# A macaron encoder layer on one core: softmax maxima and sums in one tile, new transpose banks, all attention scaling on VectorE

## The chip, the cores and the metric

The kernel is one launch on one core of a Trainium2 chip. The metric is device time in microseconds, the median of several runs. Engines are named PE (TensorE), DVE (VectorE), ACT (ScalarE), POOL (GpSimd) and SP (SyncE, which only starts transfers); PEld is the weight load of PE. Each has its own instruction queue and they meet by semaphores. All arithmetic is float32: a product of two float32 matrices is made as three passes over parts rounded to fp32r, high by high, high by low and low by high. So every operand of a product is first copied by ACT to its high part ("hi") and then subtracted by DVE to give its low part ("lo").

## The reference

```
x = x + 0.5 * post1(SwiGLU_1(pre1(x)))
h = pre_mix(x); z = h @ w_in            # pool channels | q | k | v
mixer A: centred pooling, windows 2, 4, 8, 16, minus the token, small matrix per group, scale
mixer B: dilated sliding-window attention, 3 groups of 4 heads,
         (window, dilation) = (128,1), (512,4), (2048,16), ALiBi bias
x = x + post_mix(concat(A, B) @ w_out)
x = x + 0.5 * post2(SwiGLU_2(pre2(x)))

# of one group g:
m = max(s); p = exp(s - m); den = sum(p); o = (p @ v) / den; lse = m + log(den)
# over the groups:
alpha = softmax(lse over the 3 groups); output of g = o_g * alpha_g
```

Sequence 1024, width 1024, 12 heads of 64, FFN width 2752; `post` and `pre` are RMS norms with a gain.

## The kernel before, in words

The stages follow one another: the first FFN (`gate_up(0)`, `down(0)`, up to about 625 us), the input projection in two halves of the sequence (`project_in(0)`, `project_in(1)`), the attention, the output projection, and the second FFN (`gate_up(1)`, `down(1)`). PE never waits for a stage as a whole; every engine has its list of work written out by hand, and the same lists are walked on PE, DVE and ACT.

**Attention.** There are 24 tiles n of 128 queries, 8 for each group. Tile n goes through: scores on PE (L2228), bias and maxima on DVE (`maxima`, L1500 and L1506), exponentials and their sums on ACT (`exps`, L1022), transpose on PE (`turn`, L2243), copy out of PSUM by DVE or ACT (L1519, L1032), values on PE (`values`, L2260), copy out by DVE (L1511). The maxima stand in `m_neg`, the sums in `den`, one column for a tile and head. ("step", n) in a list means: transpose tile n-2, scores of tile n, values of tile n-3. `SCHEDULE` puts steps 0 to 18 inside and behind the units of the second half of the input projection; `AFTER_IN` holds what comes behind it, steps 19 to 26 among it.

**The joint softmax.** Groups 1 and 2 have their tokens in another order, so their maxima and sums are transposed to rows, put back in natural order by the copy (`rows_`), and transposed back ("stat", b on PE L2270, its copy at L1016 or L1492, then "nat", k on PE L2312, copies at L1559 and L1560). From `nat` the coefficients follow (L1569 to L1592), those of groups 1 and 2 are transposed forth and back again (L2325, L2335), and `scale_out` (L529) multiplies the values `o_all` (a part of `vT`), once for each pair of heads and group: two by DVE, four by POOL. `turn_outputs` (L2345) transposes the scaled values; ACT and DVE copy them to `mixT`.

**Banks.** Every transpose, pool product and turned output b has a number, a PSUM bank (`TR_BANK`) and a copying engine (`TR_ON_DVE`, the others are ACT's). `tr_bank(b)` on PE waits until the last earlier b of the same bank has been copied.

**Output projection.** 24 units n, 8 slices of `w_out` for 2, then 3, then 3 tiles of tokens. For each: `hi_proj` on ACT (L720), `out_x_hi` on ACT (L1076, `mhi`), `out_w_lo` (L1193) and `out_x_lo` (L1620, `mlo`) on DVE, then 12 or 18 matmuls (L2362 to L2364) on PE. Inside these units ACT, DVE and POOL norm the finished tiles 0 to 4; `OUT_SQ1`, `OUT_NEW`, `OUT_SQ2`, `OUT_NORM` and `OUT_TURN` say behind which unit. `OUT_TURN` places the transposes `turn_x` of tiles 0 to 3 on PE (L1942), all into banks 6 and 7; ACT copies them (L784, L791) and DVE subtracts (`x_lo`, L1231) before the next may use the banks.

**Start of an FFN.** `first_steps` on DVE: weights (`lo_g`, L1175) and the four instructions of `split` for a tile (L1241 twice, L1244, L1246).

Of the kernel before, what the change touches and what calls it, by code (L numbers as in the profile page):

```python
# [6 lines left out]
F32 = mybir.dt.float32  # L7
F32R = mybir.dt.float32r
ALU = mybir.AluOpType
# [3 lines left out]
P = 128  # L13
# [121 lines left out]
OUT_SQ1, OUT_NEW, OUT_SQ2 = (7, 9, 16, 17, 19), (8, 10, 17, 18, 20), (9, 11, 18, 19, 21)  # L135
OUT_NORM, OUT_TURN = (10, 12, 19, 20, 22), (12, 15, 21, 22)
# [19 lines left out]
    (18, "mid"): [("step", 15)], (18, "end"): [("stat", 12), ("step", 16)],  # L156
    (19, "mid"): [("outw", 0), ("stat", 13), ("step", 17)], (19, "end"): [("stat", 14), ("step", 18)],
}
AFTER_IN = [("stat", 15), ("v", 12), ("step", 19), ("v", 13), ("pool", 0), ("step", 20), ("v", 14), ("pool", 1),
            ("step", 21), ("v", 15), ("pool", 2), ("pool", 3), ("step", 22), ("stat", 24), ("stat", 25), ("step", 23),  # L160
            ("nat", 0), ("step", 24), ("stat", 27), ("stat", 28), ("step", 25), ("outx", 0), ("nat", 1), ("step", 26),
            ("unit", 0)]

SCORES_FIRST = 19

# [5 lines left out]
V_NO, POOL_NO = (*range(12), 16, 17, 19, 21), (18, 20, 22, 23)  # L171
STAT_NO = {12: (1, 0, 0), 13: (1, 0, 1), 14: (1, 1, 0), 15: (1, 1, 1), 24: (2, 0, 0), 25: (2, 1, 0), 27: (2, 0, 1), 28: (2, 1, 1)}
TR_NAT, TR_ROWS, TR_COEF, TR_END = (26, 29), 30, 36, 47
TURNED_IN = {2: (34, 35), 3: (37, 38), 4: (39, 40), 5: (41, 42), 6: (43, 44), 7: (45, 46)}
TR_BANK = [4 + b % 4 for b in range(8)] + [7] * 9 + [5, 7, 5, 7, 5, 7, 5, 7, 5, 7, 5, 7, 5] + [6, 7, 4, 5] + [6, 7, 4]\
    + [5, 6, 7, 4, 5, 6, 7, 4, 5, 6]
TR_ON_DVE = (1, 3, 5, 7, 9, 11, 16, 21, 26, 28, 29, 35, 36, 38, 42, 46)
# [33 lines left out]
def layer_program(nc, io, out, xs1, xs2):  # L211
    hd = nc.dram_tensor("hd_dram", (PROD, PAIRS, P, HALF), F32).ap()
    ctx = ExitStack()
    with ctx:
# [20 lines left out]
        m_neg = sb("m_neg", [P, NTILES * HPG])  # L235
        den = sb("den", [P, NTILES * HPG])
# [61 lines left out]
        rows_ = [over(96, "rows1", [HPG, 2, SEQ]), over(0, "rows2", [HPG, 2, SEQ])]  # L298
# [213 lines left out]
        def copy_stat(copy, b):  # L512
            g, s, c = STAT_NO[b]
            copy(b, natural(rows_[g - 1][:, s, :], g, c), as_permuted(ps[0:HPG, TR_BANK[b], :], g))

        def copy_coef_rows(copy, b):
            g, c = 1 + (b - TR_ROWS) // 2, (b - TR_ROWS) % 2
            copy(b, *own_half(rows_[g - 1][:, 0, :], ps[0:HPG, TR_BANK[b], :], g, c))
# [149 lines left out]
        def _(act):  # L668
# [349 lines left out]
            def exps(n):  # L1018
                act.wait_ge(smax_done, n + 1)
                nk = P if n >= 2 * NT else 2 * P  # L1020
                for h in range(HPG):
                    a = act.activation(probs[:, n % 2, h, 0:nk], probs[:, n % 2, h, 0:nk], ACT.Exp,  # L1022
                                       bias=m_neg[:, n * HPG + h:n * HPG + h + 1],
                                       accum_out=den[:, n * HPG + h:n * HPG + h + 1])
                a.then_inc(exp_done, 1)

            def items(todo):
                for what, n in todo:
# [8 lines left out]
                    elif what == "outx":  # L1037
# [16 lines left out]
            def joint_softmax():  # L1054
                out_hi(1)
                act.wait_ge(stat_step, STAT_EXP)
                e = nat[:, 0, :, :].rearrange("p g n -> p (g n)")
                act.activation(e, e, ACT.Exp).then_inc(stat_exp, 1)
                hi_proj(OUT_U0 + 2)
# [4 lines left out]
                copy_turned(3)  # L1064
                for l in range(4, OUT_UNITS):
                    out_hi(l - 1)
                    copy_turned(l)

# [21 lines left out]
            def project_out():  # L1090
                x_load(R_MIX)
                x_load(R_MIX + 1)
                for n in range(3 * OUT_UNITS - 1):
                    if n % OUT_UNITS == OUT_UNITS - 1:
                        evac_mix(n // OUT_UNITS)
                    for i in range(HT):
# [3 lines left out]
                    if OUT_EARLY <= n + 2 < 3 * OUT_UNITS:  # L1100
                        out_hi(n + 2)
# [61 lines left out]
        def _(dve):  # L1163
# [70 lines left out]
            def split(p, i):  # L1234
# [4 lines left out]
                hi = x_split(q, 0)  # L1239
                for b, dst in enumerate(x_split(q, 1)):  # L1240
# [1202 lines left out]
```

## Time and profile before

| | |
|---|---|
| runs | 1730.39, 1730.68, 1732.2 us; median 1730.68 |
| profiled execution, its own time | 1730.15 us |
| its span | 1728.3 us, mean granted clock 0.995 |
| PE busy | 1692.5 us, 98% |
| DVE, ACT, POOL busy | 65%, 42%, 36% |

PE is busy nearly everywhere, so only three things can move the time: matmuls left out, places where PE stands still, and stretches in which its clock is halved. A busy time of the page counts an instruction's tail, which overlaps the next one: two matmuls of 512 columns start 0.227 us apart though one is given 0.39 us, and two 128-column transposes start 0.109 us apart though one is given 0.27 us. In a timeline row the number before the engine is the length of the row and the bracket gives the idle time before it and what ended it.

### The profile page before, as it was taken

How to read it: one execution, taken by the hardware profiler on the slowest of the kernel's cores; microseconds unless marked ns; L12 is line 12 of the kernel's file. 1: busy time of each engine (PE TensorE's matmuls, PEld its weight loads, DVE VectorE, ACT ScalarE, POOL GpSimd, SP SyncE). 2: the span in 40 equal slices, each digit the busy share in tenths (PEclk: the TensorE clock that was granted, in tenths of full speed). 3: DMA queues.
4: the chain of work that ended last, by engine and by line, in shares of the span. 5: the costliest groups of instructions: out<-in, count | busy, mean ns of one | idle time of the engine just before them, and what ended most of it. 6: DMA issues, size and time to landing. Idle time of an engine off the chain costs nothing. (4 is left out here: it accounts for less than half of the span.)

```text
span 1728.3 us, 21686 instructions
## 1 busy us (share of the span) xinstructions
PE 1692.5 (98%) x7949; PEld 1402.2 (81%) x7949; DVE 1116.0 (65%) x1405; ACT 717.4 (42%) x1264; POOL 621.4 (36%) x489
## 2 busy tenths in 40 slices
PE   7999999999999999999999998999999999999997
PEld 6888888888888888887887887788888888888886
DVE  7866665665668784424555767877656556647877
ACT  7432333332444553334445566533333323344453
POOL 3465554543352111118010111446545445345111
PEclk9999999999999999999999999999999999999999
DMA  6132233233853455332110256322342233484362
GB/s 216 64 116 92 92 118 132 92 100 115 316 180 101 140 152 170 119 92 84 50 50 25 67 202 183 107 88 92 111 138 93 94 114 110 152 289 144 98 232 92
DMA packets 160985, 216.98 MB, mean 126 GB/s; under 512 B 12848, under 2 KB 99056, under 8 KB 160880
## 3 DMA queue, kind: packets, MB, share of 16 engines
q1 hardware_dynamic: 153136, 188.73, 34.2%
q10 hardware_dynamic: 6896, 24.19, 4.0%
q0 software_dynamic: 848, 2.69, 0.5%
q8 instruction: 64, 1.05, 0.3%
q14 instruction: 41, 0.34, 0.1%
HBM read 162.09 MB, written 52.95 MB: 124 GB/s over the span
## 5 line engine op out<-in xcount | busy, mean ns | idle before, releaser
L2057 PE MATMUL ps<-xg,ring 128*128 128x512 f32 x1120 | 436.4, 390 | 2.3 <-DVE ring L1175 1.7
L2059 PE MATMUL ps<-xg,ring 128*128 128x512 f32 x1120 | 435.8, 389 | 0.0
L2058 PE MATMUL ps<-xg,ring 128*128 128x512 f32 x1120 | 435.7, 389 | 0.0
L2057 PEld LDWEIGHTS ps<-xg,ring 128*128 128x128 f32 x1120 | 210.2, 188 | 47.5 <-DVE ring L1175 2.5
L2059 PEld LDWEIGHTS ps<-xg,ring 128*128 128x128 f32 x1120 | 210.2, 188 | 44.0
L2058 PEld LDWEIGHTS ps<-xg,ring 128*128 128x128 f32 x1120 | 210.2, 188 | 43.1
L2120 PE MATMUL ps<-ring 128*128 128x512 f32 x616 | 240.3, 390 | 0.8 <-DVE ring L1187 0.8
L2122 PE MATMUL ps<-ring 128*128 128x512 f32 x616 | 239.7, 389 | 0.0
L2121 PE MATMUL ps<-ring 128*128 128x512 f32 x616 | 239.7, 389 | 0.0
L691 ACT ACTIVATE ring<-t_sum 128x512 fp32r<-128x512 f32 x160 | 100.3, 630 | 278.6 <-PE ps L2059 168.5
L1193 DVE TENSOR_TENSOR ring<-raw,ring 128x1024 fp32r<-128x1024 f32 x64 | 82.2, 1284 | 152.4 <-ACT ring L720 152.3
L1175 DVE TENSOR_TENSOR ring<-t_sum,ring 128x512 fp32r<-128x512 f32 x160 | 151.6, 957 | 17.9 <-ACT ring L691 17.8
L1756 POOL TENSOR_TENSOR t_sum<-raw 128x512 f32<-128x512 f32 x80 | 112.8, 1429 | 131.0 <-DVE ring L1175 114.9
L1723 POOL TENSOR_SCALAR ms<-ss 128x1 f32<-128x1 f32 x44 | 23.0, 523 | 328.7 <-ACT junk_d L755 113.1
L1778 POOL TENSOR_TENSOR u_a<-hst 128x512 f32<-128x512 f32 x40 | 66.1, 1653 | 204.5 <-DVE hst L1302 204.5
L1184 DVE TENSOR_TENSOR ring<-st_op,ring 128x1024 fp32r<-128x1024 f32 x66 | 103.9, 1574 | 51.4 <-ACT ring L702 51.2
L2120 PEld LDWEIGHTS ps<-ring 128*128 128x128 f32 x616 | 115.6, 188 | 26.0 <-DVE ring L1187 1.9
L2122 PEld LDWEIGHTS ps<-ring 128*128 128x128 f32 x616 | 115.6, 188 | 24.0
L2121 PEld LDWEIGHTS ps<-ring 128*128 128x128 f32 x616 | 115.6, 188 | 23.6
L1175 DVE TENSOR_TENSOR ring<-raw,ring 128x512 fp32r<-128x512 f32 x120 | 128.7, 1073 | 3.1 <-ACT ring L691 3.1
L2150 PE MATMUL ps<-xe,ring 128*128 128x512 f32 x320 | 127.5, 399 | 0.0
L2152 PE MATMUL ps<-xe,ring 128*128 128x512 f32 x320 | 124.9, 390 | 0.0
(220 smaller groups left out, 2781.1 us busy)
## 6 DMA issues: line engine op xcount, KB each, us to landing
st_op<-hd_dram SPq DMA_DIRECT2D x154, 256.0 KB, 2.7
raw<-in_w_gate_dram SPq DMA_DIRECT2D x20, 1024.0 KB, 6.3
raw<-in_w_up_dram SPq DMA_DIRECT2D x20, 1024.0 KB, 5.4
raw<-in_w_in_dram SPq DMA_DIRECT2D x40, 512.0 KB, 3.8
hd_dram<-u_b SPq DMA_DIRECT2D x64, 256.0 KB, 6.3
wd<-in_w_down_dram SPq DMA_DIRECT2D x18, 768.0 KB, 7.0
hd_dram<-hst SPq DMA_DIRECT2D x48, 256.0 KB, 6.3
raw<-in_w_out_dram SPq DMA_DIRECT2D x24, 512.0 KB, 3.6
```

The source lines that it names most:

```text
L691: act.activation(small(m % RING, 0), src, ACT.Copy).then_inc(hi_done, 4 if m == M_FRONT - 1 else 1)
L1175: dve.tensor_tensor(small(m % RING, 1), src, small(m % RING, 0).bitcast(F32), ALU.subtract)\
L1184: a = dve.tensor_tensor(lo, src, hi.bitcast(F32), ALU.subtract)
L1756: pool.tensor_tensor(t_tile(n, t), x, y, ALU.subtract).then_inc(t_done, 1)
L2057: pe.matmul(acc, hi[:, a, :], x_hi, start=(a == 0 and not more), stop=False, skip_group_check=more)
L2058: pe.matmul(acc, hi[:, a, :], x_lo, start=False, stop=False, skip_group_check=more)
L2059: mm = pe.matmul(acc, lo[:, a, :], x_hi, start=False, stop=(a == HALF_D - 1), skip_group_check=more)
L2120: pe.matmul(acc, s_hi, w_hi, start=(j == 0 and not top), stop=False, skip_group_check=top)
L2121: pe.matmul(acc, s_hi, w_lo, start=False, stop=False, skip_group_check=top)
L2122: return pe.matmul(acc, s_lo, w_hi, start=False, stop=(j == PAIRS - 1), skip_group_check=top)
L2150: pe.matmul(ps[:, bank, :], hi[:, a, :], x_hi, start=(a == 0), stop=False)
L2152: mm = pe.matmul(ps[:, bank, :], lo[:, a, :], x_hi, start=False, stop=(a == DT - 1))
```

## The change

1. `m_neg` and `den` become one tile `stats[P, tile, 2, head]`. One transpose carries the maxima and the sums of a tile, so that 8 "stat" entries with 4 transposes each become 4, and each "nat" has 8 transposes of 8 rows where it had 16 of 4 rows.
2. All numbers b, the banks and the copying engines are laid out anew, and `AFTER_IN` is in another order. ("stat", 15) in front of ("v", 12) is gone; there now stand ("outw", 1), DVE's and ACT's share of the weights of output unit 1, and ("nat", 0). The three parts of ("outx", 0) become ("xh", 0) on ACT and ("xl", 0) on DVE, ("unit", 0) moves ahead of step 24, and unit 1 runs between `turn_outputs(2)` and `turn_coefficients_back`.
3. The values of the last two tiles are copied by ACT (`LAST_VALUES`).
4. All six `scale_out` are on DVE, one behind each of the output units' work.
5. `OUT_*` move: tile 1 one unit earlier, the transposes of tiles 1 and 2 one unit earlier, tile 4 later; POOL works out its factors in the order 0, 1 then 2, 3 then 4.
6. At the start of an FFN `split` of the second tile is cut in two with `lo_g(p, 1)` between, and PE's unit (1, 0) waits only for the first half of it.

```diff
-OUT_SQ1, OUT_NEW, OUT_SQ2 = (7, 9, 16, 17, 19), (8, 10, 17, 18, 20), (9, 11, 18, 19, 21)
-OUT_NORM, OUT_TURN = (10, 12, 19, 20, 22), (12, 15, 21, 22)
+OUT_SQ1, OUT_NEW, OUT_SQ2 = (7, 8, 16, 17, 19), (8, 9, 17, 18, 21), (9, 10, 18, 19, 22)
+OUT_NORM, OUT_TURN = (10, 11, 19, 20), (12, 14, 20, 22)
...
-AFTER_IN = [("stat", 15), ("v", 12), ("step", 19), ("v", 13), ("pool", 0), ("step", 20), ("v", 14), ("pool", 1),
...
+AFTER_IN = [("outw", 1), ("nat", 0), ("v", 12), ("step", 19), ("v", 13), ("pool", 0), ("step", 20), ("v", 14), ("pool", 1),
+            ("step", 21), ("xh", 0), ("v", 15), ("pool", 2), ("step", 22), ("xl", 0), ("pool", 3), ("stat", 23),
+            ("step", 23), ("unit", 0), ("stat", 24), ("xh", 1), ("step", 24), ("nat", 1), ("step", 25), ("step", 26)]
...
-        m_neg = sb("m_neg", [P, NTILES * HPG])
-        den = sb("den", [P, NTILES * HPG])
+        stats = sb("stats", [P, NTILES, 2, HPG])
...
             def joint_softmax():          # ACT
-                out_hi(1)
                 act.wait_ge(stat_step, STAT_EXP)
...
+                for n in range(NTILES - LAST_VALUES, NTILES):
+                    act.wait_ge(pv_done, n + 1)
+                    act.activation(o_all[:, n, :], ps[:, 6, 0:HPG * HEAD], ACT.Copy).then_inc(o_done, 1)
...
                 scale_out(dve, 0, 0).then_inc(scaled, 1)      # DVE
+                out_x_lo(1)
                 scale_out(dve, 0, 1).then_inc(scaled, 1)
...
+                tr_copied(dve, TR_COEF)
+                scale_out(dve, 1, 0).then_inc(scaled, 1)
+                for l in range(3, OUT_UNITS):
+                    out_w_lo(l)
+                    copy_turned(l)
+                    if l < OUT_UNITS - 1:
+                        out_x_lo(l)
+                    if l < OUT_UNITS - 2:
+                        scale_out(dve, *divmod(l, 2)).then_inc(scaled, 1)
...
-            for g in (1, 2):              # POOL
-                for w in (0, 1):
-                    scale_out(pool, g, w).then_inc(scaled, 1)
...
                 split(p, 0)
-                split(p, 1)
+                split_first(p, 1)
                 lo_g(p, 1)
+                split_rest(p, 1)
...
                     if (n, k) == (1, 0):
-                        pe.wait_ge(xlo_done, Q_FFN[p] + HT + 2)
+                        pe.wait_ge(s3_done, HT * p + 2)
...
             def turn_stat(b):
...
-                    mm = pe.transpose(ps[0:HPG, bank, T * P:(T + 1) * P], (m_neg, den)[s][:, n:n + HPG], ident[:, :])
+                    mm = pe.transpose(ps[0:2 * HPG, bank, T * P:(T + 1) * P],
+                                      stats[:, n, :, :].rearrange("p s h -> p (s h)"), ident[:, :])
```

What this does to the queues, at two places. On PE, behind the second half of the input projection, the rows before are (v is `vT`, one row for four transposes; the first row is ("stat", 15)):

```order
L2270 MATMUL ps<-ident,den 4x128 x4
L2195 MATMUL ps<-ident,vT 128x128 x4
L2243 MATMUL ps<-ident,probs 128x128 x4
```

At the same place and at the end of `AFTER_IN` after the change the last statistics and the joint softmax stand like this, with unit 0 (12 rows of L2379 to L2381) just ahead of the first row:

```order
L2284 MATMUL ps<-ident,stats 8x128 x4
L2257 MATMUL ps<-ident,probs 128x128 x4
L2274 MATMUL ps<-v_nat,probsT 128x64 x4
L2326 MATMUL ps<-ident,rows 128x8 x8
L2257 MATMUL ps<-ident,probs 128x128 x4
L2274 MATMUL ps<-v_nat,probsT 128x64 x8
L2339 MATMUL ps<-ident,nat 4x128 x16
L2359 MATMUL ps<-ident,vT 128x128 x8
```

The transpose of sums that stood in front of the value transposes is gone, the transposes back are 8 and not 16, and an output unit stands among the statistics.

On DVE, from the first scaling on, before:

```order
L529 TENSOR_TENSOR vT<-vT,coef 128x8x128 x2
L1193 TENSOR_TENSOR ring<-raw,ring 128x1024
L1620 TENSOR_TENSOR mlo<-mixT,mhi 128x256
L1193 TENSOR_TENSOR ring<-raw,ring 128x1024
L1492 COPY mixT<-ps 128x512
L1492 COPY coef<-ps 128x64
L1620 TENSOR_TENSOR mlo<-mixT,mhi 128x256
L1492 COPY mixT<-ps 128x512
```

and after the change, from the copy of the coefficients (`coef`) on, two output units' worth:

```order
L1505 COPY coef<-ps 128x64
L528 TENSOR_TENSOR vT<-vT,coef 128x8x128
L1196 TENSOR_TENSOR ring<-raw,ring 128x1024
L1505 COPY mixT<-ps 128x512
L1634 TENSOR_TENSOR mlo<-mixT,mhi 128x256
L528 TENSOR_TENSOR vT<-vT,coef 128x8x128
L1196 TENSOR_TENSOR ring<-raw,ring 128x1024
L1505 COPY mixT<-ps 128x2x256
L1634 TENSOR_TENSOR mlo<-mixT,mhi 128x256
L528 TENSOR_TENSOR vT<-vT,coef 128x8x128
```

Each output unit now has four instructions in DVE's queue, weights, copy of a turned output, low part, and a scaling, where it had three at most.

## Rows read from the trace of the kernel before

**Rows 1.** The profile's page: busy time, share of the span, instructions.

```profile
PE 1692.5 (98%) x7949; PEld 1402.2 (81%) x7949; DVE 1116.0 (65%) x1405; ACT 717.4 (42%) x1264; POOL 621.4 (36%) x489
```

**Rows 2.** Waits of PE: in total, times, longest (us).

```profile
PE ps L2195 <- ACT rows L1016: 4.0, 1, 4.0
PE ps L1942 <- DVE xg L1231: 3.6, 1, 3.6
PE ps L2362 <- DVE mlo L1620: 2.1, 3, 1.2
PE ps L2057 <- DVE ring L1175: 1.7, 1, 1.7
```

**Rows 3.** Stretches of the span: length, busy time by engine, granted clock (PEclk), DMA.

```profile
943.00:990.00 47.00, 41.80 (x315) 36.21 (x314) 31.85 (x77) 26.41 (x78) 4.63 (x4) 0.93 0.19 57
...
950.60:954.02 3.42, 2.87 (x14) 2.90 (x15) 1.38 (x2) 0.41 (x1) 0.00 (x0) 0.50 0.00 0
954.02:977.92 23.90, 22.80 (x193) 19.83 (x193) 17.47 (x51) 15.96 (x54) 0.00 (x0) 1.00 0.02 3
977.92:981.33 3.41, 3.41 (x9) 2.65 (x9) 3.20 (x9) 0.90 (x1) 1.16 (x2) 0.50 0.82 222
1076.90:1080.32 3.42, 3.42 (x12) 2.83 (x11) 0.42 (x1) 2.53 (x4) 0.00 (x0) 0.50 0.07 26
```

**Rows 4.** A group of PE instructions between 943 and 990 us.

```profile
L2312 PE MATMUL ps<-ident,rows 4*128 4x4 f32 x32 | 2.2, 197 | 0.5 <-ACT rows L1016 0.5
```

**Rows 5.** Timeline behind the input projection: start, length, engine, instruction, idle before.

```profile
943.02 0.60 PE L2270 MATMUL ps<-ident,den 128*4 128x128 f32 x4
943.46 0.60 PE L2243 MATMUL ps<-ident,probs 128*128 128x128 f32 x4
...
948.41 0.40 ACT L1022 ACTIVATE probs<-probs,m_neg 128x128 f32<-128x128 f32 x1 [3.21 <-DVE m_neg L1506]
949.97 1.04 ACT L1016 ACTIVATE rows<-ps 4x512 f32<-4x512 f32 x1
951.15 1.09 PE L2195 MATMUL ps<-ident,vT 128*128 128x128 f32 x4 [3.98 <-ACT rows L1016]
952.27 0.69 DVE L1492 COPY v_nat<-ps 128x512 f32<-128x512 f32 x1 [3.89 <-PE ps L2195]
954.33 0.45 PE L2260 MATMUL ps<-v_nat,probsT 128*128 128x64 f32 x3
```

**Rows 6.** Groups of ACT, DVE and POOL instructions between 900 and 1115 us.

```profile
L720 ACT ACTIVATE ring<-raw 128x1024 fp32r<-128x1024 f32 x26 | 27.4, 1056 | 1.8 <-PE ps L2364 1.8
L1193 DVE TENSOR_TENSOR ring<-raw,ring 128x1024 fp32r<-128x1024 f32 x26 | 31.8, 1223 | 30.0 <-ACT ring L720 29.9
L529 DVE TENSOR_TENSOR vT<-vT,coef 128x1024 f32<-128x1024 f32 x2 | 2.4, 1222 | 0.0
L529 POOL TENSOR_TENSOR vT<-vT,coef 128x1024 f32<-128x1024 f32 x4 | 8.7, 2214 | 7.2 <-DVE coef L1492 7.2
```

**Rows 7.** Timeline of the output units with turned outputs, DVE.

```profile
989.49 2.13 DVE L1620 TENSOR_TENSOR mlo<-mixT,mhi 128x256 fp32r<-128x256 f32 x1
...
1005.04 0.42 DVE L1620 TENSOR_TENSOR mlo<-mixT,mhi 128x256 fp32r<-128x256 f32 x1
1005.38 1.05 DVE L1492 COPY mixT<-ps 128x512 f32<-128x512 f32 x1
```

**Rows 8.** Timeline ahead of output unit 17.

```profile
1046.46 1.08 ACT L784 ACTIVATE xg<-ps 128x512 fp32r<-128x512 f32 x2
...
1051.18 0.50 PE L2362 MATMUL ps<-ring,mhi 128*128 128x512 f32 x1 [1.17 <-DVE mlo L1620]
```

**Rows 9.** Timeline: the transposes of tile 3.

```profile
1076.34 0.99 PE L1942 MATMUL ps<-ident,y 128*128 128x128 f32 x6 [3.58 <-DVE xg L1231]
```

**Rows 10.** Timeline at the start of the second FFN.

```profile
1109.73 0.69 DVE L1246 TENSOR_TENSOR y<-ps,y 128x512 f32<-128x512 f32 x1
1111.08 0.50 PE L2057 MATMUL ps<-xg,ring 128*128 128x512 f32 x1 [1.75 <-DVE ring L1175]
```

More of the change, by code:

```diff
@@ L1238, in split @@
                 dve.wait_ge(xcopy_done, HT * p + i + 1)
-                hi = x_split(q, 0)
-                for b, dst in enumerate(x_split(q, 1)):
-                    dve.tensor_tensor(dst, x_turned(bank, b), hi[b].bitcast(F32), ALU.subtract)
+                x_second_lo(q, bank, 0)
                 if p and i >= 2:
@@ L1639, in project_out @@
                         evac_mix(n // OUT_UNITS)
-                    if OUT_EARLY <= n + 2 < 3 * OUT_UNITS:
+                    if n + 2 == OUT_EARLY:
+                        out_x_lo(n + 2)
+                    elif OUT_EARLY < n + 2 < 3 * OUT_UNITS:
                         out_lo(n + 2)
-                    for i in range(HT):
-                        if n == OUT_TURN[i]:
-                            x_lo(Q_FFN[1] + i, 6, copied=True)
                     for i in range(EARLY):
@@ L1648, in project_out @@
                             x_new(R_MIX + i)
-                        if n == OUT_NORM[i]:
+                        if i < HT and n == OUT_NORM[i]:
                             x_norm(Q_FFN[1] + i, g_pre_r)
+                    for i in range(HT):
+                        if n == OUT_TURN[i]:
+                            x_lo(Q_FFN[1] + i, 6, copied=True)
                 lo_tail(1, X_T)
@@ L1897, in _ @@
             gains(g_post_r, "g_mix_post", g_pre_r, "g_ffn2_pre")
-            pool.wait_ge(scaled, 2)
-            tr_copied(pool, TR_COEF)
-            for g in (1, 2):
-                for w in (0, 1):
-                    scale_out(pool, g, w).then_inc(scaled, 1)
-            pool.wait_ge(g_in, 64)
-            for i in range(EARLY):
-                scale_of_y(R_MIX + i)
-                scale_x(Q_FFN[1] + i)
+            pool.wait_ge(g_in, 64)
+            for tiles in ((0, 1), (2, 3), (4,)):
+                for i in tiles:
+                    scale_of_y(R_MIX + i)
+                for i in tiles:
+                    scale_x(Q_FFN[1] + i)
             for i in range(EARLY, NT):
@@ L2308, in turn_back @@
                 bank = tr_bank(b)
-                for s in range(2):
-                    for j in range(NT):
-                        n = (s * NT + j) * HPG
-                        mm = pe.transpose(ps[:, bank, n:n + HPG], rows_[k][:, s, j * P:(j + 1) * P],
-                                          ident[0:HPG, 0:HPG])
+                for j in range(NT):
+                    n = j * 2 * HPG
+                    mm = pe.transpose(ps[:, bank, n:n + 2 * HPG], rows_[k][:, j * P:(j + 1) * P],
+                                      ident[0:2 * HPG, 0:2 * HPG])
                 mm.then_inc(tr_done, 1)
@@ L2334, in turn_coefficients_back @@
                         n = (g * NT + T) * HPG
[L2335 removed]
+                        mm = pe.transpose(ps[:, bank, n:n + HPG], rows_[g][0:HPG, T * P:(T + 1) * P],
                                           ident[0:HPG, 0:HPG])
@@ L2353, in out_unit @@
                 b = out_slot(u)
-                for m in range(len(tiles)):
+                for m in (1, 0) if n == 0 else range(len(tiles)):
+                    if n == 0:
+                        pe.wait_ge(smax_done, NTILES - m)
                     if l == 0 and part and m < len(OUT_TILES[part - 1]):
@@ L2373, in project_out @@
                 turn_outputs(2)
+                out_unit(1)
                 turn_coefficients_back()
                 turn_outputs(3)
-                for n in range(1, 3 * OUT_UNITS):
+                for n in range(2, 3 * OUT_UNITS):
                     for i in range(HT):
```

100 lines of the change are left out of this document (49 added, 51 removed).

## The prediction

> **What bounds the kernel now.** I read the page first: PE is busy 1692.5 of 1728.3 us [rows 1], so nothing on DVE, ACT or POOL counts unless PE waits for it. The time can move in three ways: matmuls that go, PE's standing still, and half clock. Then the list of PE's waits [rows 2]: one of 4.0 us for ACT's copy of a statistics row, one of 3.6 for DVE's `xg`, three of together 2.1 for `mlo`, one of 1.7 for a ring weight. All four kinds lie in the attention's end, the output projection and the second FFN's start, which is where the change is. Then the stretches by clock [rows 3]: three of 3.4 us at 0.50, that is 1.2 GHz, the rest at 2.4. The first and third begin at the end of PE's two long stands (4.0 and 3.6 us), the second after a stretch in which PE was busy 22.8 of 23.9 us at full clock with small instructions. A half-clock stretch costs half of PE's busy time in it: about 1.4 us (2.87/2), 1.7 and 1.7. The rest of the kernel, some 1,500 us, keeps its instructions and its lists except the cut `split`.
>
> **Matmuls that go.** 16 of 32 statistics transposes go; a burst of four takes 943.46 - 943.02 = 0.44 us of PE [rows 5], so 4 x 0.44 = 1.8 us. Of the 32 narrow transposes back, 2.2 us [rows 4], 16 go; the others are 8 rows wide instead of 4, and I take the same price: 1.1 us. Bounds for these 16: nothing saved if the wider ones took twice as long, 1.1 if not. Sum -2.8, of which one burst (0.44) lies ahead of the first wait.
>
> **The wait before the value transposes (4.0 us) does not go; it moves.** Before, ACT copies statistics row 15 behind the exponentials of tile 18 (949.97, after 948.41), and the value transposes need that bank: 951.15 [rows 5]. Now they have bank 5 and do not wait. But the next thing that needs them, the values of tile 16, must wait until DVE has copied them, and DVE's list has got longer in front of that copy. I follow it, 0.44 earlier than before: maxima of tile 18 ready at 948.0; ACT's exponentials, 949.97 - 948.41 = 1.6, to 949.6; ACT's high part of unit 1's weights, now put here, 1.06 [rows 6], to 950.6; DVE's low part 1.22 to 951.9; the five small statistics instructions, an estimate of 0.6; the copy 0.69 [rows 5] to 953.2. The values start there and not at 954.33. PE has meanwhile done the transposes back, the value and tile transposes and scores, until about 948.9 (it came to the end of the last burst 3.98 before 951.15, which is 947.0 by start distances; less two bursts of 0.44 it is at the new list at 946.1, and the work is 0.55 + 0.44 + 0.44 + 0.89, with a moment for the maxima of tile 18), and stands 4.3 us. So the first long stand stays, with its half-clock stretch, for which I keep 1.4. What is gained is work done before it that was done later.
>
> **From there to the end of unit 1.** Before, PE's losses between 943 and 990 sum to 9.0 us: 47.0 less 41.8 of busy time is 5.2 idle [rows 3], the tails that then overlap nothing are 0.7 (0.16 each time), and half clock 1.4 and 1.7. After, by the same walking through the lists: the 4.3; two waits of 0.2 for ACT's copies of v13 and pool 0, which now queue behind the exponentials of tile 19; 0.7 in front of the values of tile 23, since DVE does the last statistics before it copies that tile's transposes; 0.8 at the coefficients and turned outputs, which wait for ACT's four row copies behind unit 2's weights (these five are estimates from the lists and the durations of rows 5 to 7, each within 0.3); half clock 1.4 once, and the second stretch with a chance of one half, 0.8. Together 8.2 to 8.4; I take 8.3. With unit 0 and unit 1 standing inside this chain, PE has real work in most of the places where the softmax's last steps run on DVE. Term: 8.3 - 9.0 - 2.8 = -3.5.
>
> **The outputs' scaling on DVE, units 2 to 7.** Each of these units takes PE 12 x 0.227 + 8 x 0.109 = 3.6 us. DVE now does for each: weights 1.22 [rows 6], copy of a turned output 1.05 [rows 7], then ACT's `mhi` 0.4 with two hand-overs of 0.05, `mlo` 0.42 [rows 7], scaling 1.22 [rows 6]: 4.4 us. DVE becomes the longer one. It starts about 1.5 us ahead, so units 2 and 3 don't wait; units 4 to 7 wait 0.45, 0.65, 0.65 and 1.1 (for the last the weights on ACT come behind `mhi` of unit 6), together 2.85, against 1.35 before. Term: +1.5. Bounds: the scaling's duration is shown on both engines, 1.22 on DVE and 2.21 on POOL [rows 6]; at POOL's price the term would be near +5, and at least 0 if the DVE instructions overlapped better. The nearest row is DVE's own. One row speaks for a gain: while POOL scaled, an `mlo` took 2.13 us and not 0.42 [rows 7]; that goes, but PE wasn't waiting for that one, so I count nothing. The Trainium skill (GPSIMD Engine Reference, "1. Specifications") says that GpSimd shares its SBUF interfaces with VectorE and contends with instructions that read two SBUF inputs; the 2.13 agrees. The same page ("4.1 Engine selection") gives two-input work on GpSimd about twice VectorE's time; 2.21 against 1.22 is 1.8. By the pages one would expect this part to gain; by the rows the order of DVE's queue decides, and it loses.
>
> **Unit 17.** Before, ACT's copies for tile 1's transposes (two of about 1.1 us, from 1046.46) stand ahead of that unit's weights, and PE waits 1.17, 1.34 with restart [rows 8]. Now these come at unit 14, before the mix is copied out, and the weights' low part would be ready at about 1049.3, before unit 16 ends at 1049.84. Term: -1.3. What is hidden there is hidden by unit 16's 4.1 us.
>
> **Tiles 2 and 3.** Before, tile 3's transposes stand behind a DVE queue of weights, norms and tile 2's `xg`: 3.58 idle [rows 9], 3.7 with restart, and half clock right behind, 1.7 [rows 3]. Now tile 2 is transposed one unit earlier, so two units of 4.1 us lie between the two and DVE is done with the banks at about 1068.5 for a need at 1072. But tile 2's norm now is what comes last: unit 18 ends, ACT makes the high part of unit 21 (1.5 us), DVE its low part (1.8), behind it the norm (1.28). That is 4.7 after the end of unit 18, and unit 19 covers 4.1: a wait of 0.7. POOL's new order (factors of tiles 2 and 3 of the mix before those of their norms) is needed for this; with the old order tile 3's new x would wait for tile 2's square. Term: -3.7 - 1.7 + 0.7 = -4.7; of the half clock I keep a chance of one in seven, +0.2: -4.5.
>
> **Start of the second FFN.** PE waits 1.75 for the second ring weight, which stands behind both `split`s on DVE [rows 10]. Two of its eight instructions now stand behind the weight: one of 0.64 (`xg`) and one of 0.69, so -1.3, at most the 1.75. Further on DVE's order is as long as it was and PE comes 1.3 earlier, so I give back 0.1. Term: -1.2. In the first FFN nothing waits there: 0.
>
> **Nothing for the rest.** ACT's copying out of the last two tiles' values, the other tile order and the moved norm of tile 4 lie beside the matmuls of units 22 and 23. SP's list isn't changed.
>
> **Sum.** -3.5 + 1.5 - 1.3 - 4.5 - 1.2 = -9.0. The profiled execution took 1730.15 (span 1728.3); it becomes 1721.1. It lies 0.5 below the median of the runs, so the same for the median: 1721.6.
>
> **Rivals.** (a) *DVE is bound in the output units*: scalings at POOL's 2.2 us or a queue that loses more at each hand-over than my 0.05. For it: three of PE's waits there were for `mlo` already [rows 2]. Against: DVE's own row of 1.22. Price +3.5: 1725.2. (b) *The wait at the transposes is exchanged for one of the same kind*: tile 2's norm is late by 3 us or more (its store must have landed, ACT's square and POOL's factor come before it), and the half clock comes back. Price +2.5 + 1.7: 1726. (c) *The waits only move*: each DVE and ACT chain keeps its end, and only the 2.8 us of matmuls and the FFN's 1.2 go: 1726.6 at best, 1729 if unit 0's new place costs what it gives. (d) *Slower*: half clock holds over the whole stretch from the first stand to the coefficients, about 22.8 us of busy time [rows 3], which would cost 22.8 more and leave 1721.6 + 22.8 - 2.2 (already counted) = 1742. It decides from five more half-clock stretches of 1.7 on. Against it: before, the very same kinds of instruction ran at 1.00 for 23.9 us. The Trainium skill (TensorE: Matmul & The Clock Gate, "Part 4: PE-mode transpose") says that transposes don't count as busy for the clock; by that rule the stretch would have run slowly before as well, so the trace doesn't bear it out as a rule for the whole, though it may be why 977.92 was slow.
>
> **Chances.** The forecast, 1719 to 1724: 0.68. (a) 0.11, (b) 0.09, (c) 0.08, (d) 0.04. Of the range's ends: low, both the uncertain half-clock stretches away, no wait for tile 2 and the FFN's whole 1.75, 1721.6 - 0.8 - 0.2 - 0.7 - 0.5 = 1719.4, and as much again for waits that I overrate (the 4.3 can't go, the 2.85 can): 1717.5. High, (a) and (b) in: 1727. What the measurement tells from no change is 0.2%, 3.5 us: faster is the forecast and most of (a) and (b), 0.86; same is the rest of them and (c), 0.09; slower 0.05.
>
> **What would show it.** In the profile after: a PE wait of about 4.3 us on DVE's `v_nat` copy (not on ACT's rows), with a half-clock stretch behind it; no PE wait over 1 us at tile 3's transposes and no half clock there, a wait under 1 us at tile 2's; `mlo` waits growing from 2.1 to 3 us or more, all in units 4 to 7; the FFN's ring wait down to about 0.5. It would be wrong if the long wait at `v_nat` were gone, if DVE's scalings took over 1.3 us each, or if PE's clock fell more than three times.

## The result, and the profile after

The changed kernel took 1721.39 us (median of 4, 1720.69 to 1722.04) beside 1731.15 for the kernel before on the same chip (4 runs, 1730.39 to 1732.20). The ratio is 0.9943, 95% interval 0.9926 to 0.9960, so the change gains 9.8 us. The profiled execution took 1721.88 (span 1720.1), 8.3 less than that of before; the other three runs had spans of 1718.9 to 1719.3.

The page's busy times, to be read against [rows 1]: PE is busy 2.9 us less, with 32 instructions fewer, and its share is still 98%.

```profile
PE 1689.6 (98%) x7917; PEld 1399.1 (81%) x7917; DVE 1118.5 (65%) x1408; ACT 714.8 (42%) x1261; POOL 618.2 (36%) x485
```

PE's waits after (line, engine and tile waited for: us in total, times, longest), against [rows 2]. `...` stands for rows left out; `uu` is DVE's first combination of PE's results in an FFN:

```profile
PE ps L2274 <- DVE v_nat L1505: 3.9, 1, 3.9
PE ps L2379 <- DVE mlo L1634: 1.5, 4, 0.7
...
PE ps L2071 <- DVE uu L1289: 1.0, 2, 0.8
...
PE ps L2274 <- ACT vT L1058: 0.6, 1, 0.6
...
PE ps L2071 <- DVE ring L1178: 0.5, 2, 0.3
```

The long wait has another name (the copy of values, not the statistics row) and the same length. The 3.6 us at tile 3 are gone, the mlo waits went down from 2.1 to 1.5 because unit 17's 1.2 is no longer among them (those of units 2 to 7 rose from 0.9 to 1.5), and uu has grown (its two waits together were 0.4 before). The stretches of the changed kernel that answer to [rows 3], with the granted clock in the third column from the right, show the rest:

```profile
943.00:990.00 47.00, 42.30 (x292) 35.59 (x291) 30.58 (x74) 24.96 (x75) 1.16 (x2) 0.89 0.17 57
951.20:958.03 6.83, 4.93 (x17) 3.82 (x18) 4.14 (x14) 2.52 (x10) 0.00 (x0) 0.50 0.00 1
958.03:978.51 20.48, 19.91 (x152) 17.34 (x151) 15.02 (x43) 12.24 (x43) 0.00 (x0) 1.00 0.08 27
978.51:981.92 3.41, 3.41 (x18) 2.15 (x18) 3.40 (x4) 2.86 (x5) 1.16 (x2) 0.50 0.45 109
987.59:1010.27 22.68, 21.18 (x107) 16.79 (x106) 18.79 (x22) 12.21 (x17) 0.00 (x0) 1.00 0.49 163
1040.00:1080.00 40.00, 39.88 (x184) 32.92 (x183) 31.45 (x37) 25.46 (x40) 8.43 (x12) 1.00 0.57 179
```

Two stretches at 0.50 (1.2 GHz) in which PE works are left of three, but the first is now 6.83 us long. (In both kernels the clock falls once more behind PE's last matmul, where it costs nothing.) In the last row, which holds units 16 to 23 and the transposes of tiles 2 and 3, PE is busy for 39.88 of 40.00 us at 2.4 GHz: nothing there stands or runs slowly any more.

I compare the two kernels by where PE starts fixed pieces of work. The second column is what the prediction said, the third the difference of the profiled executions:

| piece of PE's list | predicted | measured |
|---|---|---|
| up to the start of unit 2 (989.72 before, 987.59 after) | -3.5 | -2.1 |
| units 2 to 7 (21.62 us before, 22.68 after) | +1.5 | +1.1 |
| unit 8 to the start of unit 17 | -1.3 | -1.2 |
| unit 17 to the end of unit 23, with tiles 2 and 3 | -4.5 | -5.1 |
| from there to the end | -1.2 | -0.8 |
| sum, before rounding | -9.0 | -8.3 |

**The long stand.** The timeline of the changed kernel ahead of the wait (start, length, engine, instruction, idle before) is the chain that the prediction followed:

```profile
947.90 0.40 ACT L1021 ACTIVATE probs<-probs,stats 128x128 f32<-128x128 f32 x1 [3.21 <-DVE stats L1519]
...
949.45 1.04 ACT L719 ACTIVATE ring<-raw 128x1024 fp32r<-128x1024 f32 x1
950.52 1.23 DVE L1196 TENSOR_TENSOR ring<-raw,ring 128x1024 fp32r<-128x1024 f32 x1 [2.66 <-ACT ring L719]
951.67 0.26 DVE L1580 COPY nat<-stats 128x32 f32<-128x32 f32 x2
...
952.16 0.68 DVE L1505 COPY v_nat<-ps 128x512 f32<-128x512 f32 x1
...
953.10 1.94 PE L2274 MATMUL ps<-v_nat,probsT 128*128 128x64 f32 x8 [3.85 <-DVE v_nat L1505]
```

DVE stands 2.66 us for ACT's high part of unit 1's weights while the copy that PE needs, 0.68 long, is queued behind. PE goes on at 953.10, where 953.2 was forecast.

**Output units.** A unit of DVE's queue, the rows that answer to [rows 7]:

```profile
994.82 0.42 DVE L1634 TENSOR_TENSOR mlo<-mixT,mhi 128x256 fp32r<-128x256 f32 x1 [0.53 <-ACT mhi L1077]
995.16 1.22 DVE L528 TENSOR_TENSOR vT<-vT,coef 128x1024 f32<-128x1024 f32 x1
996.29 1.22 DVE L1196 TENSOR_TENSOR ring<-raw,ring 128x1024 fp32r<-128x1024 f32 x1
997.43 1.07 DVE L1505 COPY mixT<-ps 128x512 f32<-128x512 f32 x1
999.03 0.43 DVE L1634 TENSOR_TENSOR mlo<-mixT,mhi 128x256 fp32r<-128x256 f32 x1 [0.53 <-ACT mhi L1077]
```

From one mlo to the next it is 4.2 us (forecast 4.4), for 3.6 of PE's work. No mlo takes 2.13 us any more.

**Start of the second FFN.** PE's two waits there, which answer to [rows 10]:

```profile
1102.17 0.50 PE L2071 MATMUL ps<-xg,ring 128*128 128x512 f32 x1 [0.30 <-DVE ring L1178]
...
1144.99 0.47 PE L2071 MATMUL ps<-xg,ring 128*128 128x512 f32 x1 [0.82 <-DVE uu L1289]
```

By start-to-start distances the first lost 1.91 us before and 0.46 now; the second lost 0.36 before and 0.99 now.

### The profile page after: what moved, and what is told of

The parts are those of the page before. It is cut to its first block and busy times, and to the rows that moved or that the text cites. A ratio compares the mean times of both kernels' runs of the same rounds, so it can differ in the third digit from the quotient of the medians.

```text
span 1720.1 us, 21614 instructions
## 1 busy us (share of the span) xinstructions
PE 1689.6 (98%) x7917; PEld 1399.1 (81%) x7917; DVE 1118.5 (65%) x1408; ACT 714.8 (42%) x1261; POOL 618.2 (36%) x485
```

## The experiments

Each kernel was timed in three to five rounds beside the kernel before, whose median was 1731.69, 1731.98 and 1732.18 us in the three groups (e1 to e4, e5 to e8, e9 to e12). The changed kernel itself stands at 1721.39. Since the medians of before differ by up to 1.0 us between groups, a difference of 1 or 2 us between two changed kernels is taken as shown only where their traces show it in the piece that was edited.

**e1_out_order.** The kernel before with the moves around units 7 to 23 alone:

```diff
-OUT_SQ1, OUT_NEW, OUT_SQ2 = (7, 9, 16, 17, 19), (8, 10, 17, 18, 20), (9, 11, 18, 19, 21)
-OUT_NORM, OUT_TURN = (10, 12, 19, 20, 22), (12, 15, 21, 22)
+OUT_SQ1, OUT_NEW, OUT_SQ2 = (7, 8, 16, 17, 19), (8, 9, 17, 18, 21), (9, 10, 18, 19, 22)
+OUT_NORM, OUT_TURN = (10, 11, 19, 20), (12, 14, 20, 22)
...
-            for i in range(EARLY):
-                scale_of_y(R_MIX + i)
-                scale_x(Q_FFN[1] + i)
+            for tiles in ((0, 1), (2, 3), (4,)):
```

The rows left out above also change the order inside the units: ACT makes the weights' high part ahead of its copies of the transposes, and DVE norms ahead of `x_lo`.

> The kernel before with part 5 alone (the places of the norms and transposes inside the output units, ACT's order there, POOL's order of factors). Theory: the terms for unit 17 and for tiles 2 and 3 stand by themselves, -1.3 and -4.5 to -5.0, so 6 us less than the kernel before: about 1725.0, no PE wait over 1 us between 1040 and 1100 us and no half clock there. Rival: the gain there needs the earlier parts of the change too (the units then come earlier or later against the transfers), under 3 us here.

Measured: 1724.52 us (1722.87 to 1724.70), ratio 0.9956, interval 0.9941 to 0.9971. Unit 8 to the start of unit 17 is 1.3 us shorter and unit 17 to the end of unit 23 is 5.15 shorter, as in the changed kernel. The waits of 1.2 and 3.6 us are off PE's list, and no half clock stands behind tile 3. These two pieces need nothing of the rest of the change, and their 6.4 us are three quarters of the 8.3. The span of this execution is only 5.5 less than that of before (1722.8 for 1728.3), because unit 8 starts 0.8 later than before; the medians are 7.2 apart.

**e2_split.** The kernel before with the cut split alone:

```diff
                 split(p, 0)
-                split(p, 1)
+                split_first(p, 1)
                 lo_g(p, 1)
+                split_rest(p, 1)
...
-                        pe.wait_ge(xlo_done, Q_FFN[p] + HT + 2)
+                        pe.wait_ge(s3_done, HT * p + 2)
```

> The kernel before with part 6 alone (the second tile's split cut in two, unit (1, 0) waiting for its first half). Theory: 1.2 to 1.45 us come back at the FFN's second unit, but the FFN's first sums (uu) then wait longer, 0.6 us as in the changed kernel, so 0.6 to 0.9 us net. Rival: the longer wait for uu in the changed kernel comes from something else (the profile of one execution), then 1.3 us net and the uu wait stays at 0.2.

Measured: 1730.87 us (10 runs), ratio 0.9997, interval 0.9988 to 1.0006: no change that can be measured. PE's two waits in its timeline:

```profile
1109.72 0.50 PE L2067 MATMUL ps<-xg,ring 128*128 128x512 f32 x1 [0.29 <-DVE ring L1175]
...
1152.83 0.47 PE L2067 MATMUL ps<-xg,ring 128*128 128x512 f32 x1 [1.12 <-DVE uu L1286]
```

The weight's wait has gone from 1.75 to 0.29, as calculated, and 40 us later PE waits 1.12 for uu where it waited 0.2. PE's unit came 1.36 us earlier (1109.72 for 1111.08), the chain in front of uu only 0.44. In the changed kernel it reads so, POOL, ACT and DVE in turn:

```profile
1131.98 1.50 POOL L1789 TENSOR_TENSOR hst<-u_a,hst 128x512 f32<-128x512 f32 x1 [4.03 <-DVE xg L1270]
...
1140.90 1.29 POOL L1773 TENSOR_TENSOR t_sum<-t_sum,raw 128x512 f32<-128x512 f32 x1 [0.62 <-DVE ring L1178]
1142.28 0.63 ACT L690 ACTIVATE ring<-t_sum 128x512 fp32r<-128x512 f32 x1 [8.92 <-POOL t_sum L1773]
1142.95 0.69 DVE L1178 TENSOR_TENSOR ring<-t_sum,ring 128x512 fp32r<-128x512 f32 x1 [2.13 <-ACT ring L690]
1143.56 0.68 DVE L1178 TENSOR_TENSOR ring<-raw,ring 128x512 fp32r<-128x512 f32 x1
1144.16 0.68 DVE L1289 TENSOR_TENSOR uu<-ps,m1b 128x512 f32<-128x512 f32 x1
```

Five sums on POOL of 1.7 us each run beside four low parts on DVE that take 6.88 us there, where the four before them took 2.5. POOL's last sum waits for DVE's weight behind these, ACT for that sum, and uu for both. Against the kernel before this chain lies 0.44 us earlier in e2 (uu at 1151.99 for 1152.43), and e2's span is shorter by the same 0.44 (1727.9 for 1728.3). The medians differ by 0.8, less than the spread of either kernel's runs, so this gain is read from one trace and isn't shown in the time.

**e3_pool_scales.** The changed kernel, the scalings of groups 1 and 2 on POOL as before:

```diff
-                scale_out(dve, 1, 0).then_inc(scaled, 1)
...
-                        scale_out(dve, *divmod(l, 2)).then_inc(scaled, 1)
...
+            for g in (1, 2):              # POOL
+                for w in (0, 1):
+                    scale_out(pool, g, w).then_inc(scaled, 1)
```

> The changed kernel with the four scalings of groups 1 and 2 back on POOL. Theory: DVE's queue sets the waits of units 4 to 7 (1.5 us by the list of waits, 2.1 by start distances); without the scalings it has 3.2 us of work a unit and the waits fall to at most the 1.3 of the kernel before: 0.8 to 1.5 us less than the changed kernel. Rival: the waits come from the chain copy on DVE, high part on ACT, low part on DVE, whatever else is in the queue, and from DVE slowed by POOL; then no change or slower by up to 1 us.

Measured: 1721.42 us (1721.00 to 1721.68), ratio 0.9942. Units 2 to 7 take 22.71 us, for 22.68 with DVE. The groups of that stretch show why nothing was won (columns: shapes and count | busy us, mean ns | idle before):

```profile
L1196 DVE TENSOR_TENSOR ring<-raw,ring 128x1024 fp32r<-128x1024 f32 x6 | 10.2, 1695 | 1.9 <-ACT ring L719 1.9
...
L528 POOL TENSOR_TENSOR vT<-vT,coef 128x1024 f32<-128x1024 f32 x4 | 9.7, 2460 | 7.0 <-DVE coef L1505 7.0
...
L1630 DVE TENSOR_TENSOR mlo<-mixT,mhi 128x256 fp32r<-128x256 f32 x5 | 2.7, 546 | 2.7 <-ACT mhi L1077 2.7
```

DVE is rid of four scalings of 1.22 (4.9 us), but its own two-input instructions lengthen while POOL works: the six weights take 10.2 us and not 7.3, the low parts 2.7 and not 2.1. Seen in one instruction:

```profile
995.03 2.45 DVE L1196 TENSOR_TENSOR ring<-raw,ring 128x1024 fp32r<-128x1024 f32 x1 [0.41 <-ACT ring L719]
```

POOL's four scalings ran from 986.66 to 996.39 in this trace; the weights and low parts behind 999 have their 1.23 and 0.42 again. So 3.5 of the 4.9 us come back while POOL works, and of the rest DVE idles more for ACT's weights (1.9 us, for 1.0 in the changed kernel). The Trainium skill (GPSIMD Engine Reference, "1. Specifications") says that GpSimd and VectorE share SBUF interfaces for such instructions; 2.45 against 1.22 agrees. What I had concluded from it, that the move to VectorE gains, does not follow here: the time is the same in either place.

**e4_early_weights.** The changed kernel with unit 1's weights taken out of the chain of the long stand:

```diff
-    (19, "mid"): [("outw", 0), ("stat", 12), ("step", 17)], (19, "end"): [("stat", 13), ("step", 18)],
+    (19, "mid"): [("outw", 0), ("stat", 12), ("step", 17)], (19, "end"): [("stat", 13), ("wh", 1), ("step", 18)],
...
-AFTER_IN = [("outw", 1), ("nat", 0), ("v", 12), ("step", 19), ("v", 13), ("pool", 0), ("step", 20), ("v", 14), ("pool", 1),
+AFTER_IN = [("v", 12), ("wl", 1), ("nat", 0), ("step", 19), ("v", 13), ("pool", 0), ("step", 20), ("v", 14), ("pool", 1),
```

So that DVE may copy the value transposes first, the numbers of these transposes and of the first transposes back change places too.

> The changed kernel with ACT's high part of unit 1's weights ahead of step 18, where ACT stands idle, and the copy of value transposes 12 ahead of DVE's low part and of the first statistics. Theory: the 3.9 us stand of PE for v_nat is DVE's queue behind exponentials and weights; it falls under 1 us, and the half-clock stretch of 6.8 us behind it goes too: 4 to 6 us less than the changed kernel, about 1716.5. Rival: the stand is only exchanged for one at tile 17's transposes or tile 19's scores (exponentials of tile 18 are no earlier), at least 2 us of it stays, and the clock falls as before: under 2.5 us less.

Measured: 1716.73 us (1715.90 to 1717.77), ratio 0.9914, interval 0.9899 to 0.9928. Between 940 and 985 us PE waits for this now, in place of 3.9 us for v_nat:

```profile
PE ps L2209 <- ACT v_nat L1015: 0.8, 1, 0.8
PE ps L2274 <- ACT vT L1058: 0.6, 1, 0.6
PE ps L2242 <- DVE stats L1519: 0.3, 1, 0.3
```

The long stand is gone, and so is the half-clock stretch of 6.83 us behind it: the clock is 1.00 up to 973.32. A stretch of 3.41 us is still there from then on, as in the row below (e4, columns as in [rows 3]), and unit 2 starts at 982.43, 5.2 us earlier than in the changed kernel:

```profile
973.32:976.73 3.41, 3.41 (x18) 2.15 (x18) 3.38 (x5) 2.80 (x5) 1.17 (x2) 0.50 0.31 107
```

**e5_no_scaling and e6_copies_on_act.** Two ways to shorten DVE's queue in units 2 to 7. e5 leaves out the four scalings of groups 1 and 2, so their outputs stay unscaled, and PE no longer waits for them; in e6 only the table of DVE's copies changes (the second cut below), so that ACT makes the last four copies:

```diff
-                scale_out(dve, 1, 0).then_inc(scaled, 1)
...
-                    if l < OUT_UNITS - 2:
-                        scale_out(dve, *divmod(l, 2)).then_inc(scaled, 1)
```

```diff
-TR_ON_DVE = (1, 3, 5, 7, 9, 11, 14, 15, 20, 25, 31, 32, 34, 36, 38, 40, 42)
+TR_ON_DVE = (1, 3, 5, 7, 9, 11, 14, 15, 20, 25, 31, 32, 34)
```

> The changed kernel with the four scalings of groups 1 and 2 left out (the outputs of these groups stay unscaled). It asks what the waits of output units 4 to 7 (.37, .49, .43 and .86 us in the changed kernel's trace, with 22.7 us from the start of unit 2 to the start of unit 7's work) stand on. Theory A, the working of the prediction: DVE's queue is too long by the scaling of 1.22 us for each unit. Without it DVE has 2.7 us of work for 3.6 us of PE, the waits of units 4 to 7 go but for a part of unit 7's (its weights stand on ACT behind mhi of unit 6): 1720.0, the waits for mlo together under 0.5. Rival B: the chain of copy, high part and low part sets them, whoever scales (scaling on POOL changed nothing): waits stay at 2 us together and the time at 1721.4.

> The changed kernel with the copies of the last four turned-output pairs (units 4 to 7) made by ACT and not by DVE. Theory A (DVE's queue sets the waits of units 4 to 7): DVE loses 1.05 us for each unit and ACT, which has 1.06 for weights and 0.4 for mhi, takes some 1.1: the waits of units 4 to 6 go, 1.3 us together, and the time is 1720.2. Rival B (the chain copy, mhi, mlo sets them): the copy is on the chain wherever it is made, and it now stands behind ACT's weights: waits equal or longer, 1721.4 to 1723.

Measured: 1718.77 us (1717.44 to 1719.57) and 1718.96 (1718.71 to 1719.31), ratios 0.9925 and 0.9926. Units 2 to 7 in e5, then in e6 (length, busy time of PE, PEld, DVE, ACT, POOL, clock):

```profile
986.63:1006.66 20.03, 20.03 (x108) 16.86 (x107) 14.49 (x18) 12.61 (x17) 0.00 (x0) 1.00 0.57 176
```

```profile
986.72:1006.96 20.24, 20.24 (x108) 16.70 (x106) 14.94 (x18) 16.10 (x21) 0.00 (x0) 1.00 0.56 174
```

PE has no wait left in either, and the six units are 2.65 and 2.4 us shorter than the changed kernel's 22.68. Rival B is out: the length of DVE's queue decides, and unit 7's wait went with the others. In the medians both gain 2.6 and 2.4 us, where I had expected 1.4 and 1.2, half of it: I let a part of unit 7's wait stay, and took the waits without the 0.1 or so that PE loses at each restart beside them.

**e12_scaling_in_gap.** The changed kernel, DVE's scaling put where DVE idles for ACT's mhi:

```diff
                     copy_turned(l)
+                    if l < OUT_UNITS - 2:
+                        scale_out(dve, *divmod(l, 2)).then_inc(scaled, 1)
                     if l < OUT_UNITS - 1:
                         out_x_lo(l)
-                    if l < OUT_UNITS - 2:
-                        scale_out(dve, *divmod(l, 2)).then_inc(scaled, 1)
```

> The changed kernel; in units 3 to 5 DVE's scaling stands between the copy of a turned output and the low part mlo, and not behind mlo. In the changed kernel's trace DVE idles there 0.54 us for each unit, for ACT's mhi (2.7 in units 2 to 7). Theory A (what counts is the sum of DVE's queue with its idle time): the scaling fills the idle time, 0.5 us for each of three units: 1720.3. Rival B (the chain copy, mhi, mlo counts): mlo comes 0.7 later for each, waits grow: 1722.5 to 1723.5.

Measured: 1720.08 us (1719.31 to 1720.51), ratio 0.9931. DVE's idle time for mhi in units 2 to 7 fell from 2.7 us to 1.1:

```profile
L1634 DVE TENSOR_TENSOR mlo<-mixT,mhi 128x256 fp32r<-128x256 f32 x5 | 2.1, 418 | 1.1 <-ACT mhi L1077 1.1
```

The six units take 21.07 us, 1.6 less; in the medians it is 1.3. Same instructions, another order: DVE's idle time inside the queue counts as its work does.

**e7_fill_matmuls and e8_fill_transposes.** The changed kernel, with PE kept busy in the long stand, by matmuls in e7 and by transposes in e8. Nothing reads their results.

```diff
+                        if n == SCORES_FIRST:
+                            for _ in range(16):
+                                pe.matmul(ps[:, 2, :], xe[1][:, 0, 4, 0:P], xe[1][:, 0, 5, :], start=True, stop=True)
```

```diff
+                        if n == SCORES_FIRST:
+                            for _ in range(32):
+                                pe.transpose(ps[:, 2, 0:P], ident[:, :], ident[:, :])
```

> The changed kernel with 16 extra matmuls of 512 columns (3.6 us at full clock) on PE behind the last scores, where PE stands 3.9 us for the copy of the values of tile 16. Their results are used by nothing. Theory A: the long stand is what takes the clock to 0.50 behind it (6.83 us there, and 3.41 at 978 as well). With PE busy the half-clock stretch of 6.83 goes; if both go, some 2.5 + 1.6 us are won less what the fill is too long for (0.2): 1717.5 to 1719. Rival B: the lower clock comes from the small instructions that follow: both stretches stay and the time is 1721.4 or up to 0.5 more.

> The same place filled with 32 transposes of 128 columns (3.5 us) in place of matmuls; their results are used by nothing. If transposes keep the clock as matmuls do: the same time as with the matmuls, 1717.5 to 1719, no half clock near 951. If transposes do not count for the clock, as the Trainium skill states (TensorE: Matmul & The Clock Gate, Part 4: PE-mode transpose), the stretch of half clock stays, and since the filling itself may then run at half clock for a part of its length, the time is 1721.4 to 1724.

Measured: 1719.16 us (1718.39 to 1719.87) and 1719.45 (1718.49 to 1719.49), ratios 0.9927 and 0.9928. The stretch of the first row of the windows above, in e7:

```profile
943.00:990.00 47.00, 45.73 (x328) 38.97 (x327) 33.39 (x78) 27.06 (x78) 1.16 (x2) 1.00 0.20 65
```

and in e8, up to its only half-clock stretch, and that stretch:

```profile
943.00:975.70 32.70, 31.49 (x250) 27.84 (x248) 22.20 (x63) 18.81 (x65) 0.00 (x0) 1.00 0.06 17
975.73:979.14 3.41, 3.41 (x18) 2.31 (x18) 3.34 (x6) 2.38 (x5) 1.16 (x2) 0.50 0.32 76
```

More work on PE, and the kernel is 2 us faster: the stand takes the clock down, and what follows it pays. Against the changed kernel, unit 2 starts 3.5 us earlier in e7 and 2.5 in e8. Transposes did it as well as matmuls: the clock stayed at 1.00 through 3.5 us of them and behind them. The Trainium skill (TensorE: Matmul & The Clock Gate, "Part 4: PE-mode transpose") says that transposes don't count as busy for the clock, by which the stretch behind them would be slow; this trace doesn't agree, for these transposes of 4-byte numbers. What this shows is the first stretch. The second was still there in the trace of e8, and in that of e4, neither of which has a stand of more than 0.8 us before it, and it was missing in e7 but also in e5 and e6, which have the stand of 3.9. So the second stretch does not hang on the stand, and what brings it stays open.

**e9_combine_first.** The changed kernel; to free uu of DVE's queue:

```diff
+                    if m == 8:
+                        for e in (1, 2, 3):
+                            combine(p, 0, e)
                     lo_g(p, m + 4)
...
-                    if m in (8, 9):
+                    if m == 9:
                         for e in (1, 2, 3):
-                            combine(p, m - 8, e)
+                            combine(p, 1, e)
```

> The changed kernel; in the first steps of each FFN, DVE's three combinations of unit 0 stand ahead of the low part of the next ring weight and not behind it. It asks where the gain of the cut split went: PE's wait for the second weight fell by some 1.3 us, but its wait for the first combination (uu, 1144 us) rose by as much less .5. Theory A: that combination is held by DVE's queue alone, behind a weight whose sum POOL makes last (its bank is full at 1141.3, it runs at 1144.2): the wait of 0.8 at uu goes and nothing takes its place: 1720.4. Rival B: the ring weight that now stands behind the combinations is late in its turn: the wait only changes its name, 1721.4, or 1722 if it grows.

Measured: 1721.83 us (1721.21 to 1722.13), ratio 0.9942. PE's timeline:

```profile
1143.82 0.47 PE L2074 MATMUL ps<-xg,ring 128*128 128x512 f32 x1 [0.22 <-DVE uu L1289]
...
1147.21 0.47 PE L2074 MATMUL ps<-xg,ring 128*128 128x512 f32 x1 [0.43 <-DVE uu L1289]
```

By start distances these lose 0.38 and 0.59 us, together 0.96, for 0.99 in one wait before. The time is that of rival B, though the second wait is for unit 1's `uu`, which now stands behind the weight, and not for the weight itself. The edit also missed its aim in part: the weight whose sum POOL makes last (on DVE at 1142.38) still stands ahead of uu (1142.99); uu was moved past the next weight only. Whether taking uu past both would pay wasn't tried.

**e10_weights_and_copies and e11_all_three.** e10 is e4 and e6 together, e11 adds e9's order.

> The changed kernel with two edits together: unit 1's weights early (the weights' high part before the statistics of tile 19, the low part behind the copy of the values of tile 16) and the copies of the last four turned-output pairs on ACT. If the two are independent, each as measured alone (-4.7 and -2.4): 1714.3. If they share a loss (the copies wait for what the weights have let go, ACT's queue is now behind in unit 2): 1715.5 to 1716.7.

> The same with DVE's combinations of unit 0 ahead of the ring weight too. By theory A of that edit another 1.0 less: 1713.3; by its rival the same as the two edits: 1714.3.

Measured: 1715.65 us (1714.31 to 1716.28), ratio 0.9906, and 1714.12 (1713.08 to 1714.38), ratio 0.9897, interval 0.9883 to 0.9912. The order of e11 was taken in although e9 had gained nothing alone. In the profiled executions units 2 to 7 are 2.3 us shorter in e10 than in e4, as in e6 against the changed kernel (2.4), but e10 had a half-clock stretch of 6.83 us at 972.51 where e4 had one of 3.41. In e11 PE's clock stayed at 1.00 there:

```profile
943.00:1001.50 58.50, 56.66 (x386) 47.84 (x385) 42.66 (x89) 40.12 (x95) 1.16 (x2) 1.00 0.32 102
```

From the end of unit 23 to the end e10 and e11 take the same 640.52 us, so e11's lead of 1.5 in the medians does not come from what its order does there; in the traces it is the clock. That the order caused the better clock is not shown; nothing of it lies ahead of 1001 us but in the first FFN. e11 is the fastest kernel here, 18.1 us under the kernel before in its group, and 7.3 under the changed one.

## Why the prediction was right, and where its steps were off

**The sum** was -9.0; the profiled difference is -8.3 and that of the medians -9.8. Four of five terms came within 0.6 us and the fifth missed by 1.4. That the median of 1721.39 lies 0.2 from the 1721.6 forecast is luck in part: the terms' misses partly cancel, and the profiled execution of before was 1.0 under its median, where that of the change was 0.5 above.

**Up to unit 2: -3.5 forecast, -2.1 measured; the half clock was mis-sized.** The chain of the long stand was right to 0.1 us (953.10 for 953.2). By start distances 2.7 us of transposes went, for 2.8 forecast: 4 bursts of 0.435, and the transposes back cost 2 x 0.585 where they cost 2 x 1.05. The step that failed is "half clock 1.4 once, and the second stretch with a chance of one half, 0.8". In the trace the first stretch cost 4.93/2 = 2.5 and the second 3.41/2 = 1.7, 4.2 in place of 2.2. The waits were overrated beside it: PE idles 4.7 us between 943 and unit 2 (0.28, 3.85 and 0.56), 5.2 with the tails, where the five waits of the forecast sum to 6.2. The two waits of 0.2, and the 0.8 at the coefficients and turned outputs, are not on PE's list there. So 1.0 too much for the waits hid half of the 2.0 too little for the clock.

The clock behind this stand isn't the same from kernel to kernel. Six traces have the same lists from the input projection up to 980 us, with the same stand of 3.9. In the changed kernel, e5 and e6 the first stretch is 6.83 us long and begins while PE stands (951.20, 951.58, 951.91). In e3, e9 and e12 it is 3.41 and begins 0.1 to 0.8 us after PE works again (954.03, 953.65, 953.41). The second came in four of the six, not in e5 and e6. Unit 2 starts at 986.63 and 986.72 in e5 and e6, at 987.02, 987.01 and 987.05 in e3, e9 and e12, and at 987.59 in the changed kernel's profiled run, the only one with both the long first stretch and the second. The middle of them is 2.7 before the 989.72 of the kernel before. In e7, with neither stretch, unit 2 starts at 984.08.

**Units 2 to 7: +1.5 forecast, +1.1 measured.** DVE's queue as the bound was right (e5, e6, e12); the hand-overs were a little cheaper (4.2 us a unit, not 4.4). The sign that I named for it was wrong, though: I wanted mlo waits of 3 us or more on PE's list, and it shows 1.5. The list counts less than PE loses: from start to start the six units lost 2.65 us against e5. What the prediction had wrong in this part is the comparison with POOL: it gave a term of "near +5" at POOL's price and counted nothing for the lengthened mlo. Its count for the kernel before was low as well: 1.35 us of waits, where the six units took 1.6 more than e5's 20.03. e3 shows the two places to be worth the same, since POOL's scaling slows DVE's queue by nearly as much as its own would.

**Unit 17: -1.3 forecast, -1.2 measured,** and e1 gives -1.3 for it alone.

**Tiles 2 and 3: -4.5 forecast, -5.1 measured.** Tile 2's norm was to be 0.7 late; the loss at its unit is 0.3 by start distances (PE's transposes at 1061.39 start 0.28 late), and in the changed kernel's trace the clock did not fall there.

**The second FFN: -1.2 forecast, -0.8 measured; a gain that was given back.** The step "so I give back 0.1" failed: the wait for the weight fell by 1.45, and uu's grew by 0.63. The chain in front of uu runs through POOL's sums and ACT and moved by 0.44 when PE's unit moved by 1.36 (e2), so PE arrives earlier and waits. In e2, where this part stands alone, that takes all of the gain but 0.5.

**The rivals.** (a) was the mechanism of the forecast at a higher price, and the price did not come. (b) and (c) did not occur. (d), half clock over the whole stretch, did not occur either: 958.03 to 978.51 ran at 1.00 with PE busy 19.91 of 20.48 us.

## What to carry to other kernels

When a wait is taken away at the head of a long chain, look for the next wait whose releaser hangs on other engines: PE that is 1.3 us earlier wins nothing if POOL's sums aren't. Ask of each stand what it leaves behind it, since the stretch after it at 1.2 GHz cost up to two thirds of the stand again (2.5 for 3.85). Here it was worth more to take one weight out of the chain of such a stand (-4.7 us) than to choose another engine for the scaling (0) or the copies (-2.4). Before moving work between DVE and POOL, price it with both running: twice the time on POOL and DVE slowed meanwhile may sum to the same, and a slot in which the queue idles anyway, or ACT, is the better place.

## What was not expected of the hardware

- Behind the same stand of 3.9 us the half-clock stretch was 6.83 us in three traces and 3.41 in three others, with the same lists from the input projection up to there: long where it began within the stand, short where it began after it. A second one came in four of the six, and in e4, e8 and e10 with no stand of more than 0.8 us before it; what brings it is open.
- 3.5 us of unused transposes in that stand kept the clock at 1.00 just as unused matmuls did.
- A two-input DVE instruction of 128x1024 took 2.45 us while POOL ran one of its own, for 1.22 alone; four of 128x512 on DVE beside POOL's sums took 6.88 us, for 2.5 alone, and POOL's sums lasted 1.7.
- The 8-row transposes back cost PE nearly what the 4-row ones did: 0.585 us for a burst of 8, for 1.05 for a burst of 16, 0.065 and 0.061 from one start to the next.
